# Hybrid decoder layer on one core: a weight sum of the down-projection kept in DRAM, the last steps reordered, part of the last rows formed on TensorE

## The reference, cut to what matters

```
h = gelu(gate) * val                 # (512, 5632), from the up-projection and a causal convolution
f = h @ w_down                       # (512, 5632) @ (5632, 2048)
out = x1 + f * rsqrt(mean(f * f, axis=-1) + 1e-6) * g_ffn_post
```

## Time and profile before

| | |
|---|---|
| median of the executions shown | 2064.72 us |
| profiled execution | 2064.49 us |
| its span, first to last instruction | 2062.7 us |
| TensorE busy | 1998.8 us, 97% |
| VectorE busy | 1545.6 us, 75% |
| ScalarE busy | 1012.3 us, 49% |
| DMA queue of SyncE, packets' time as a share of 16 engines | 45.0% |
| granted TensorE clock, mean | 0.993 of full |

### The profile page before, as it was taken

The page is one execution under the profiler, slowest core; times in us unless marked ns, Lnnn a source line. Parts: engine busy times, 40 slices in busy tenths (PEclk is TensorE's granted clock), DMA queues, the critical chain, the costliest instruction groups (busy, mean ns, idle before and its releaser), DMA issues.

```text
span 2062.7 us, 31761 instructions
## 1 busy us (share of the span) xinstructions
PE 1998.8 (97%) x12510; PEld 1796.4 (87%) x12510; DVE 1545.6 (75%) x2028; ACT 1012.3 (49%) x1549; POOL 0.7 (0%) x6
## 2 busy tenths in 40 slices
PE   8999999999999889999999999999999999999994
PEld 6888888888887789999999999999999787878773
DVE  5522543445446889898898889888998998899998
ACT  7422433435435655555555555545555554554442
POOL 0000000000000000000000000000000000000000
PEclk9999999999999999999999999999999999999998
DMA  8433232211636534324423432442344776668793
GB/s 317 138 123 118 77 93 82 82 62 62 244 124 211 177 103 160 119 100 151 149 101 121 163 117 100 136 163 101 111 145 154 237 245 211 224 214 295 254 361 125
DMA packets 218895, 323.26 MB, mean 157 GB/s; under 512 B 9134, under 2 KB 140622, under 8 KB 216444
## 3 DMA queue, kind: packets, MB, share of 16 engines
q1 hardware_dynamic: 218076, 315.99, 45.0%
q10 hardware_dynamic: 672, 5.24, 0.6%
HBM read 292.60 MB, written 32.54 MB: 158 GB/s over the span
## 4 chain that ended last, share of the span: by engine, by line
PE 83%; DVE 10%; issue 3%; ACT 3%; DMA 1%; DVEq 0%; SPq 0%; ACTq 0%
PE ring L2034 11%; PE ring L2036 11%; PE ring L2035 11%; PE ring L2295 9%; PE ring L2297 9%; PE ring L2296 9%; PE side L2295 4%; PE side L2297 4%; PE side L2296 4%; PE side L2034 2%; PE side L2035 2%; PE side L2036 2%; DVE w_lo L1721 2%; DVE raw L1730 1%; PE side L2110 1%
## 5 line engine op out<-in xcount | busy, mean ns | idle before, releaser
L1442 DVE TENSOR_TENSOR w_lo<-raw,w_hi 128x512 fp32r<-128x512 f32 x256 | 169.7, 688 | 275.2 <-ACT w_hi L1027 275.2
L1721 DVE TENSOR_TENSOR w_lo<-q,w_hi 128x1024 fp32r<-128x1024 f32 (+1 forms) x262 | 308.3, 1177 | 79.7 <-ACT w_hi L1244 69.5
L2295 PE MATMUL ring<-s_hi,w_hi 128*128 128x256 f32 x1008 | 286.8, 284 | 6.7 <-ACT snaps L1336 3.5
L2296 PE MATMUL ring<-s_lo,w_hi 128*128 128x256 f32 x1008 | 286.4, 284 | 0.0
L2297 PE MATMUL ring<-s_hi,w_lo 128*128 128x256 f32 x1008 | 286.4, 284 | 0.0
L1721 DVE TENSOR_TENSOR w_lo<-raw,w_hi 128x1024 fp32r<-128x1024 f32 x214 | 249.3, 1173 | 37.1 <-ACT w_hi L1244 26.9
L1027 ACT ACTIVATE w_hi<-raw 128x512 fp32r<-128x512 f32 x256 | 151.8, 624 | 187.7 <-PE ring L2036 171.1
L1244 ACT ACTIVATE w_hi<-q 128x1024 fp32r<-128x1024 f32 x174 | 183.6, 1056 | 97.5 <-PE side L2297 54.2
L2295 PEld LDWEIGHTS ring<-s_hi,w_hi 128*128 128x128 f32 x1008 | 194.8, 193 | 7.3 <-ACT snaps L1336 3.9
L2295 PE MATMUL ring<-a_hi,w_hi 128*128 128x256 f32 x688 | 195.3, 284 | 4.0 <-issue 3.3
L2034 PE MATMUL ring<-w_hi,act_hi 128*128 128x512 f32 x488 | 192.9, 395 | 3.3 <-DVE w_lo L1442 2.7
(11 more groups left out here) (298 smaller groups left out, 4672.8 us busy)
## 6 DMA issues: line engine op xcount, KB each, us to landing
q<-in_w_up SPq DMA_DIRECT2D x65, 1024.0 KB, 5.0
q<-in_w_down SPq DMA_DIRECT2D x66, 512.0 KB, 4.5
raw<-in_w_down SPq DMA_DIRECT2D x66, 512.0 KB, 4.5
raw<-in_w_in SPq DMA_DIRECT2D x28, 1024.0 KB, 5.4
raw<-in_w_out SPq DMA_DIRECT2D x24, 1024.0 KB, 4.9
raw<-in_w_up SPq DMA_DIRECT2D x23, 1024.0 KB, 6.9
q<-sa_d SPq DMA_DIRECT2D x22, 512.0 KB, 4.4
raw<-in_w_mem_kv SPq DMA_DIRECT2D x8, 1024.0 KB, 7.1
```

The lines of the kernel that those rows point to most:

```text
L1442: dve.tensor_tensor(w_lo[:, s, q], raw[:, s, q], w_hi[:, s, q].bitcast(F32), ALU.subtract).then_inc(lo_done, 1)
L1721: dve.tensor_tensor(lo, src, hi.bitcast(F32), ALU.subtract).then_inc(hp_lo_done, 1)
L2295: pe.matmul(dst, hi, b_hi, start=first, stop=False, skip_group_check=True)
L2296: pe.matmul(dst, hi, b_lo, start=False, stop=False, skip_group_check=True)
```

## The change

It does the following.

- The steps of passes 0 and 1 load B11 and B22 beside B12 so that one DVE operation of 128x1024 forms both T3 and T1 (before: two of 128x512, the second waiting for the first).
- After that operation SP writes T3 (256 KB) to DRAM (`spill_t3`), in the window after `load_down(d + 3)`. The load into that slot (`load_down(d + 4)`) waits until the write has landed.
- The steps of passes 2 and 3 load T3 from DRAM, B11 and B21 (three DMAs of 256 KB instead of two of 512 KB), and form T2 = T3 + B11 in one operation instead of two. T4 is formed as before.
- In passes 0 and 1 the first half of a step now forms p3 and p7, the second p1 and p5. At the pass ends ACT copies three products out instead of one (`keep`), two in the old window and `bank_x` one window later; the sums of DVE move into the later window.
- The last four steps are run by half first, then by `m`: p6 and p2 for `m = 0`, for `m = 1`, then p4 for `m = 0`, for `m = 1`.
- The last rows: the mean square of the `f0` part is prepared by a small DVE operation beside each `times_gain`, the square root takes it as a bias. DVE finishes the `f1` half only. The `f0` half is formed on TensorE in float32: a diagonal matrix of the reciprocal roots (made by ACT in one 128x128 buffer `diag`) times `f0`, plus the identity times `x1`, in PSUM, for each tile two banks of 512 columns; ACT copies the banks to `f0`, from where SP sends them off.

The core of the diff (declarations, semaphores and the table of operands in `sum_f` are left out; there the sums are regrouped, with the same number of eight for each pass end):

```diff
-        + [(1, what, m) for m in range(2) for what in ("11", "12", "22", "21b", "21")])
+        + [(1, what, m) for m in range(2) for what in ("11", "12", "22", "21b")] + [(1, "21", 0), (1, "21", 1)])
+KEEPS = [(n, what, m) for n in range(2) for what in ("21", "12", "11") for m in range(2)]
...
-TAIL_T = (0, 2, 1, 3)
+TAIL_T = (0, 1, 2, 3)
...
-                def both(at, k):
-                    sp.dma_start(seg(d, at, 2).rearrange("p (b n) -> p b n", b=2),
-                                 w_down_d[k, :].rearrange("k (b n) -> k b n", b=2)[:, :, n1]).then_inc(down_in[s], 16)
-
                 if v < 2:
-                    both(0, k1)
-                    sp.dma_start(seg(d, 2), w_down_d[k2, n2]).then_inc(down_in[s], 16)
-                else:
-                    both(2, k1)
-                    both(0, k2)
+                    if d >= 4:
+                        sp.wait_ge(t3_out[s], 16 * (d // 4))
+                    sp.dma_start(seg(d, 2, 2).rearrange("p (b n) -> p b n", b=2),
+                                 w_down_d[k1, :].rearrange("k (b n) -> k b n", b=2)[:, :, n1]).then_inc(down_in[s], 16)
+                    sp.dma_start(seg(d, 0), w_down_d[k2, n2]).then_inc(down_in[s], 16)
+                else:
+                    k = p if v == 2 else 2 * N_PAIRS - 1 - p
+                    sp.wait_ge(t3_out[k % 4], 16 * (k // 4 + 1))
+                    if 2 * N_PAIRS <= d < 2 * N_PAIRS + 4:
+                        sp.wait_ge(t3_out[s], 16 * ((d - 4) // 4 + 1))
+                    sp.dma_start(seg(d, 1), t3_d[v % 2, p]).then_inc(down_in[s], 16)
+                    sp.dma_start(seg(d, 3), w_down_d[k1, n1]).then_inc(down_in[s], 16)
+                    sp.dma_start(seg(d, 0), w_down_d[k2, n1]).then_inc(down_in[s], 16)
+
+            def spill_t3(d):
+                v, p = pass_pair(d)
+                sp.wait_ge(block_sum, block_sum_count(d, "T3"))
+                sp.dma_start(t3_d[v, p], seg(d, 1)).then_inc(t3_out[d % 4], 16)
...
@@ -975,6 +997,9 @@
                 if e % 2 == 0 and 4 <= e // 2 < N_STEP:
                     sp.wait_ge(hp_lo_done, H_DOWN + e - 6)
                     load_down(e // 2)
+                e = w - H_DOWN + 4
+                if e >= 0 and e % 2 == 0 and e < 4 * N_PAIRS:
+                    spill_t3(e // 2)
...
-            for i, t in enumerate(TAIL_T):
-                for n in range(2):
-                    sp.wait_ge(out_ready, 2 * i + n + 1)
-                    sp.dma_start(out_d[:, t, :].rearrange("p (h n c) -> p h n c", h=2, n=2)[:, :, n, :],
-                                 f_row(n, t)).then_inc(out_done, 16)
+            for n, t in ((1, 0), (1, 1), (0, 0), (1, 2), (0, 1), (0, 2), (1, 3), (0, 3)):
+                if n:
+                    sp.wait_ge(out_ready, t + 1)
+                else:
+                    sp.wait_ge(row_kept, 2 * t + 2)
+                sp.dma_start(out_d[:, t, :].rearrange("p (h n c) -> p h n c", h=2, n=2)[:, :, n, :],
+                             f_row(n, t)).then_inc(out_done, 16)
...
                 if w in (w_at(0), w_at(1)):
+                    for what in ("21", "12"):
+                        for m in range(2):
+                            keep(w == w_at(1), what, m)
+                if w in (w_at(0) + 1, w_at(1) + 1):
                     for m in range(2):
-                        keep(w == w_at(1), m)
+                        keep(w == w_at(1) + 1, "11", m)
...
+            def row_root(t):
+
+                act.wait_ge(mean_ready, t + 1)
+                act.wait_ge(f_squared, TT + t + 1)
+                act.activation(root[:, NB_F + t, 0:1], ssq_f[:, t, 1:2], ACT.Sqrt, bias=mean0[:, t:t + 1],
+                               scale=1.0 / D).then_inc(root_ready, 1)
+
+            def row_out(t):
+
+                if t > 0:
+                    act.wait_ge(row_added, 2 * t)
+                act.wait_ge(rstd_ready, NB_F + t + 1)
+                act.activation(diag[:, :], ident[:, :], ACT.Copy, scale=rstd[:, NB_F + t, 0:1]).then_inc(diag_ready, 1)
+                for h in range(2):
+                    act.wait_ge(row_added, 2 * t + h + 1)
+                    act.activation(f0[:, t, h, :], row_bank(t)[h][:, :], ACT.Copy).then_inc(row_kept, 1)
+
+            for t in range(3):
                 f_square(1, t)
-                take_root(NB_F + i, 1)
+                row_root(t)
+            row_out(0)
+            f_square(1, 3)
+            row_root(3)
+            for t in range(1, TT):
+                row_out(t)
...
-                plus(d, 3, 1, 2)
-                dve.wait_ge(block_sum, block_sum_count(d, "T3"))
-                plus(d, 1, 1, 0)
+                halves = raw_slots[d % 4].rearrange("p (b h n) -> p b h n", b=2, h=2)
+                b12 = seg(d, 3)
+                dve.tensor_tensor(halves[:, :, 1, :], halves[:, :, 0, :], both_times(b12), ALU.add).then_inc(block_sum, 1)
...
-                plus(d, 3, 3, 2)
-                dve.wait_ge(block_sum, block_sum_count(d, "T1"))
                 plus(d, 1, 1, 3)
...
-                if w == w_at(0) or w == w_at(1):
-                    sum_f(w == w_at(1), "12a", 0)
-                    sum_f(w == w_at(1), "12a", 1)
                 if w == w_at(0) + 1 or w == w_at(1) + 1:
                     n = w == w_at(1) + 1
-                    for m in range(2):
-                        sum_f(n, "22a", m)
-                        sum_f(n, "21a", m)
                     sum_f(n, "12b", 0)
                     sum_f(n, "12b", 1)
+                    for m in range(2):
+                        sum_f(n, "21a", m)
+                        sum_f(n, "22a", m)
+                    sum_f(n, "12c", 0)
+                    sum_f(n, "12c", 1)
...
+                    dve.tensor_scalar(mean0[:, k:k + 1], ssq_f[:, k, 0:1], 1.0 / D, EPS, ALU.mult,
+                                      ALU.add).then_inc(mean_ready, 1)
...
+            for m in range(2):
+                dve.wait_ge(down_ready, m + 1)
+                for what in ("11", "12", "22", "21b"):
+                    sum_f(1, what, m)
+                times_gain(TT + m, 1, m)
+                if m == 1:
+                    dve.wait_ge(down_ready, 3)
+                    sum_f(1, "21", 0)
+                finish(m)
+            times_gain(TT + 2, 1, 2)
+            dve.wait_ge(down_ready, 4)
+            sum_f(1, "21", 1)
+            finish(2)
+            times_gain(TT + 3, 1, 3)
+            finish(3)
...
+                    kept = {(1, "p7"): (0, "21"), (1, "p3"): (0, "12"), (1, "p1"): (0, "11"),
+                            (2, "p6"): (1, "11"), (2, "p4"): (1, "21"), (3, "p6"): (1, "12")}.get((v, name))
+                    last = {(1, "p5"): (0, "22a"), (2, "p2"): (1, "22a"), (3, "p2"): (0, "11"),
+                            (3, "p4"): (0, "21b")}.get((v, name))
+                    if kept:
+                        pe.wait_ge(f_kept, keep_count(*kept, m))
+                    if last:
+                        pe.wait_ge(f_summed, sum_count(*last, m))
...
-                half, at = {"p1": (0, 0), "p5": (0, 1), "p7": (1, 1), "p3": (1, 0),
+                half, at = {"p3": (0, 0), "p7": (0, 1), "p1": (1, 0), "p5": (1, 1),
...
-            for m in range(2):
-                for half, names in ((0, ("p6", "p2")), (1, ("p4",))):
+            for half, names in ((0, ("p6", "p2")), (1, ("p4",))):
+                for m in range(2):
                     for d in range(N_STEP - 4, N_STEP):
                         if m == 0:
                             operands(d, half)
                         for name in names:
                             mm = down_product(d, name, m)
                     mm.then_inc(down_ready, 1)
+            pe.wait_ge(x1_back, 16 * TT)
+            for t in range(TT):
+                pe.wait_ge(diag_ready, t + 1)
+                for h in range(2):
+                    if t == 0:
+                        pe.wait_ge(f_summed, sum_count(0, "21", h))
+                        pe.wait_ge(f_gained, TT)
+                    elif t == 1:
+                        pe.wait_ge(f_summed, sum_count(1, "11", h))
+                    else:
+                        pe.wait_ge(row_kept, 2 * t - 3 + h)
+                    pe.matmul(row_bank(t)[h][:, :], diag[:, :], f0[:, t, h, :], start=True, stop=False)
+                    pe.matmul(row_bank(t)[h][:, :], ident[:, :], x1_back_at[:, t, h * D // 2:h * D // 2 + BLK],
+                              start=False, stop=True).then_inc(row_added, 1)
```

More of the change, by code:

```diff
@@ L439, in build @@
         rden = sb("rden", [P, N_TASKS])
+        diag = sb("diag", [P, P])
         sinks = sb("sinks", [P, A_HEADS])
@@ L531, in build @@
         down_in = [sem(f"down_in{i}") for i in range(4)]
+        t3_out = [sem(f"t3_out{i}") for i in range(4)]
+        mean_ready, diag_ready, row_added, row_kept = (sem("mean_ready"), sem("diag_ready"), sem("row_added"),
+                                                       sem("row_kept"))
         x1_back, g_f_in = sem("x1_back"), sem("g_f_in")
@@ L670, in blocks_in @@
```

(46 more changed lines are left out.)

52 lines of the change are left out of this document (25 added, 27 removed).

## The result

The changed kernel takes 2100.96 us (median of four executions, 2100.2 to 2102.56), the kernel before beside it 2065.46: ratio 1.0173, 95% interval 1.0155 to 1.019. It is slower by 35.5 us. The forecast was 2075.5 us with a range up to 2087: the side was right and the place of the loss too, but the size, 11.0 us of span, was a third of the 35.8 that came.

A forecast was written before the change was run, and what follows sets the result against it. TensorE was taken to bound the kernel, with 83% of the chain. Terms 13.3 (T3 loop) - 1.0 (end of pass 2) - 3.1 (pass 3) + 1.8 (tail) = +11.0 us: span 2073.7, time 2075.5 us, range 2060 to 2087.

The forecast's parts named there:

- The write of T3 and what queues behind it: SP's queue, passes 0 and 1: each load waits for T3's landing, rounds outlast steps, loads fall behind; +13.3 us.
- if 0.3 longer, 10 come: Range of the loop term: each of 33 rounds 0.3 us longer adds 10 us, 0.3 shorter removes 10.
- The pass end from load 46: End of pass 1: load 46 issued at 1852.0 us, landing about 5 later, 3.8 us of DVE work, p2 at 1860.8.
- the loop closes in time: Rival for SP's queue, passes 0 and 1: rounds some 0.45 us shorter, total -3.0 us, time 2061.5 us; chance 0.23.
- sums: DVE, passes 0 and 1: one operation for two saves 0.19 us per step, covering both pass 0 waits; -1.6 us.
- pass ends: TensorE's waits at the ends of passes 0, 1 and 2, had loads been in time: -0.5, +1.4 and -1.0 us.
- pass 3: Pass 3 and last operands: DVE needs 4.4 us per step instead of 4.90, stretched steps and small waits go; -3.1 us.
- tail: Last four steps to span end: serial rows of 4.8 us on ACT and TensorE, 46.9 us instead of 45.1; +1.8 us.
- The clock rival: Tail: last three rows at 1.2 GHz with the loop harmless, 10.3 us more, time 2071.8 us; chance 0.07.

The follow-up runs named there:

- e1: Changed kernel with one wait moved: DVE's sum, not the load, waits for T3's landing of four steps earlier; 2066.36 us, ratio to the kernel before 1.0004.
- e3: Kernel before plus only the write of T3 to DRAM, with the load four steps later waiting for its landing; 2108.35 us, ratio 1.0208.
- e5: e1 with the products of step 0 alone back in the order p1, p5, p7, p3; 2061.91 us, ratio to the kernel before 0.9981.
- e8: Changed kernel, loop closed, with only the order of products in step 0 as before; 2102.12 us, ratio to the kernel before 1.018.
- e6: e5 without rows on TensorE: DVE finishes both halves of each tile, last steps in the new order; 2050.33 us, ratio to the kernel before 0.9929.
- e4: Kernel before plus the same T3 writes, with DVE's sum four steps later, not the load, waiting for the landing; 2065.71 us, ratio 1.0002.
- e9: e5 with two diag buffers, identity product first, and f0 of tiles 2 and 3 on DVE; 2052.4 us, ratio to the kernel before 0.9936.

## Why the prediction was right in its mechanism and wrong in its size

**The write of T3 and what queues behind it: right in place, mis-sized.** The loop was there in every round, and undoing it alone gave back 34.6 us (e1); adding it alone to the kernel before cost 43.4 (e3). The step that failed is the term of +13.3 us for the loop, +13.9 at the first p2, where the runs show +37.8. It was built from the length of a round and from a start on time at load 13, and both were wrong (in the table a range gives the shortest and the longest round):

| round | forecast, us | measured, us |
|---|---|---|
| first three of the loop (loads 4 to 7) | not in the sum | 8.16, 7.95, 6.9 |
| 512 KB operand ahead of the write | 6.9 | 7.53 (mean of 8) |
| 384 KB ahead | 6.5, with a second item behind 6.7 | 6.9 to 7.7, with a second item 7.4 and 7.6 |
| operand behind the write | 5.5 | 5.3 to 6.9 |
| clean | 5.3 | 5.3 to 5.7, one of 6.7 |
| load 13 to 24 | 62.2 | 66.0 |
| load 24 to 46 | 138.4 | 151.3 |

With load 13 going out 7.2 us later than forecast, load 46 went out at 1875.89 instead of 1852.0 us: 23.9 us, nearly the whole miss of 24.8 in the span (+35.8 against +11.0). In the rounds with 512 KB the 0.6 us that I lacked lie in the landing of the operand. I had it 6.2 us after the first issue of the round (1.4 + 4.8); it was 6.65 to 6.95, since it landed 5.2 to 5.6 us after its own issue. The write landed 0.7 us behind it, as I had taken, so a write was no dearer than I thought (the load of 3.7 us that I set beside it is one of the quiet stretch; in the stretch of those writes the second load took 4.3). What is new in the round is the write behind the operand. e3 has the loads and their order as in the kernel before, and there too the second load lands after 4.7 and 4.8 us and the operand after 5.5 to 5.9 (median of each tile, 1740 to 1786 us), where the kernel before has 3.9 to 4.3 and, but for one of 6.7, 4.8 to 5.0 (1731 to 1759 us). So it is likely that the write delays what was asked for just ahead of it; my sum let only the write wait. Over the 33 rounds from load 13 on the excess is 0.5 us each (217.3 against 200.6), outside a range of 0.3. I named this lever ("if 0.3 longer, 10 come") and then let the range end at it.

**The first rounds: not in the sum.** I started the loop's account at load 13 with the loads on time. The loop begins at load 4, and two of the first three rounds have an operand ahead of the write. The 7.2 us at load 13 are three parts: load 4 itself goes out 2.4 us later than before (1600.13 against 1597.70), the way from load 4 to load 13 takes 2.8 us more (58.5 against 55.65), and the 1.95 us of DVE's savings that I had counted do not come.

**Where it is paid: earlier than I said.** I expected DVE to meet unlanded weights from about step 38 and TensorE to bear some 7 us within pass 1. DVE met them from step 16, and TensorE was 30.3 us late at the last matmul of pass 1. The sum up to p2 could still be made from load 46 alone, because by then the loads bound every step.

**The pass end from load 46: right.** Forecast 8.8 us from load 46 to p2 of pass 2, measured 8.85, with the links that I had listed: landing 5.0 us after the issue, sum of step 46 at 1880.88, a low part, then DVE's sums of the banks until 1884.7.

**The start of pass 0: missed, and without effect.** The new order of products waits for the bank of p3: 0.88 and 2.71 us, then half speed. In the open kernel this costs 4.5 us (e1 against e5); in the changed kernel nothing (e8), because the loads set the time.

**The other terms.** With the loop open and step 0 as before, e5 takes 2061.9 us; the rival *the loop closes in time* had 2061.5, so the total of sums, pass ends, pass 3 and tail was right (-3.0 forecast, -3.9 against the kernel before beside e5). Part of that is luck, since errors of opposite sign cancel: the pass ends came out 1.3 us better than forecast, the tail of e5 0.5 worse. In e1 the three pass ends cost, beyond the pitch of the matmuls, 1.5, 3.5 and 1.5 us where the kernel before has 2.6, 2.7 and 2.6 (the longest of them in the earlier trace rows): -1.1, +0.8 and -1.1 against -0.5, +1.4 and -1.0 forecast. Behind p2 of pass 2 the changed kernel gained 2.0 us of the 2.9 forecast, although the granted clock was 0.95 from 1880 to 1970 us.

**The tail: right, and the better question not asked.** A row took 4.7 us (forecast 4.8), one at half speed 6.4; ACT's rows of the changed kernel for two tiles:

```profile
2085.64 0.39 ACT L1465 ACTIVATE diag<-ident,rstd 128x128 f32<-128x128 f32 x1
2088.10 0.60 ACT L1468 ACTIVATE f<-side 128x512 f32<-128x512 f32 x1 [2.07 <-PE side L2469]
...
2090.31 0.39 ACT L1465 ACTIVATE diag<-ident,rstd 128x128 f32<-128x128 f32 x1
```

From the start of the last four steps to the end: 47.6 us (forecast 46.9, before 45.1). The tail as a whole looked harmless at +1.8 only because its two parts cancel: the new order of the last steps, with what was made ready for the rows, is worth 9 us (e6 needs 36.0), and the serial rows on TensorE cost 11 (e5 needs 47.4). I had written that DVE ends long before, and did not ask what it could do in that time.

**The clock rival.** In the changed kernel one row of four fell to half speed (it followed a wait of 2.4 us; behind the same wait in e5 the row kept full speed) and cost 1.7 us; it never was the 10 us of that rival. The Trainium skill (page "TensorE: Matmul & The Clock Gate", section "HAM oscillation — how this bites in real kernels") describes a kernel whose short bursts of matmuls alternate with longer waits for DMA and which starts every burst slow. The trace agrees where a wait was long: behind the 6.55 us at the end of pass 1 the matmuls came 0.43 us apart, half speed. Short waits rarely did this: of eleven waits of 0.6 to 2.6 us between 1728 and 1866 us three were followed by some 3 us at half speed (granted clock 0.96 in pass 1), and in e1 the stretch from 2014 to 2050 us, with two waits of 2 us between the last steps and the gaps between the rows, has a granted clock of 1.00.

## What to carry to other kernels

When a queue's program waits for the landing of a transfer issued in the same round, the round's length is that transfer's landing behind everything asked for ahead of it; compare it with the step's length, and price it by landings read behind a queue as full as it will be. What a round is longer than the step adds up once per step; here 0.5 us of error in the round became 17 us in 33 rounds. Start the account at the first round of the loop. Ask first which instruction truly overwrites the data, and put the wait there; failing that, issue the awaited write ahead of the loads, so that it is a round old when it is awaited. When the order of products changes, look at both ends of the stage: the bank of the first product must be free as well.

## What the runs showed that I had not expected

- 11.5 MB more of writes to DRAM in some 250 us, on top of the 230 GB/s of the kernel before, cost no time that can be told (e4: 1.0002 [0.9993, 1.0011]). They do cost landings: in e4 the second load of a step lands after 5.5 to 6.0 us (1735 to 1765 us) where the kernel before has 3.9 to 4.1 (1727 to 1760 us). The lead of the loads over DVE's sums, 14.6 us at step 24 before, takes that up.
- Moving a 512 KB transfer from ahead of a 256 KB write to behind it shortens the write's round by 1.6 us (7.53 to 5.91), with the same bytes.
- Six outputs of 512 KB asked for within 4.5 us move at 305 to 326 GB/s and the last lands after 5.4 us; spread out, each lands after 3.0 to 3.2. A tail can be shortened on the engines and get nothing for it (e9).
- An operation with a repeated operand (`both_times`, 128x1024) took 1.23 us, as one without.
